# Gates applied ahead of the down product, expert rows added to x by accumulating DMAs, the sample tokens' out product in four column groups, and constant matmuls in the routing

## What is computed

```
pg = softmax(hf @ w_rg + b_rg); gi = argmax(pg); gp = pg[gi]
le_sel = (hf @ w_re + b_re).reshape(N, 4, 8)[gi]
top_p, top_i = top_k(softmax(le_sel), 2); top_p = top_p / sum(top_p)
gates = gp * one_hot(gi) * within(top_p, top_i)
a = einsum('nd,edf->nef', h, w_gate)
b = einsum('nd,edf->nef', h, w_up)
hid = silu(a) * b * gates[:, :, None]
moe = einsum('nef,efd->nd', hid, w_down)
y = rmsnorm(x + moe(rmsnorm(x, ln2_g)), lnf_g)
```

## Time and profile before

| | |
|---|---|
| median of 3 runs | 454.67 us (454.48 to 455.6) |
| profiled execution | 453.13 us |
| its span, first to last instruction | 451.2 us |
| mean granted TensorE clock | 0.929 |
| busy: PE, DVE, ACT, POOL | 378.4, 222.2, 151.7, 70.8 us |
| DMA | 109.14 MB, mean 242 GB/s |

### The profile page before, as it was taken

How to read it: one execution, slowest core, us unless ns; L and a number is a source line. 1 busy time by engine, 2 the same in 40 slices (tenths; PEclk the granted TensorE clock), 3 DMA queues, 4 the chain that set the end, 5 groups by cost and what they waited for, 6 DMA issues and landing times. The chain is left out here.

```text
span 451.2 us, 5978 instructions
## 1 busy us (share of the span) xinstructions
PE 378.4 (84%) x2256; PEld 193.8 (43%) x2256; DVE 222.2 (49%) x438; ACT 151.7 (34%) x322; POOL 70.8 (16%) x59
## 2 busy tenths in 40 slices
PE   1999996699799899999989999717999999999100
PEld 1554542244344334446544465515655555554000
DVE  2967356969765656347361234571122222222196
ACT  5823122034425436444441135502122222222042
POOL 0000303643350100000000000211233232221100
PEclk9999998889899999999999999956999999999655
DMA  8973321874900474910019996579999999995384
GB/s 292 361 210 98 138 93 52 269 267 140 368 27 0 134 249 143 295 69 2 1 49 397 410 410 271 202 276 388 358 395 410 412 410 409 408 403 229 129 332 170
DMA packets 42321, 109.14 MB, mean 242 GB/s; under 512 B 7864, under 2 KB 8632, under 8 KB 42288
## 3 DMA queue, kind: packets, MB, share of 16 engines
q1 hardware_dynamic: 36000, 94.78, 57.0%
q0 software_dynamic: 5856, 12.81, 7.7%
q10 hardware_dynamic: 432, 1.11, 0.7%
HBM read 100.00 MB, written 16.94 MB: 259 GB/s over the span
## 5 line engine op out<-in xcount | busy, mean ns | idle before, releaser
L1493 PE MATMUL bank<-weights_split,tokens_split 128*128 128x512 f16 (+1 forms) x744 | 175.1, 389 | 2.9 <-DVE x L1223 1.4
L1493 PEld LDWEIGHTS bank<-weights_split,tokens_split 128*128 128x128 f16 (+1 forms) x744 | 70.2, 98 | 94.7 <-issue 18.5
L620 POOL TENSOR_TENSOR big<-big,middle 128x1536 f32<-128x1536 f32 x8 | 28.2, 3531 | 100.4 <-DMA middle<-sample_q 50.9
L1764 PE MATMUL bank<-big,tokens_split 128*64 128x256 f32 x320 | 38.3, 394 | 1.6 <-ACT tokens_split L915 1.6
L1399 DVE TENSOR_TENSOR middle<-bank,middle 128x128 f32<-128x128 f32 x16 | 4.7, 293 | 58.5 <-ACT middle L920 58.5
L1764 PEld LDWEIGHTS bank<-big,tokens_split 128*64 128x64 f32 x320 | 23.6, 142 | 13.3 <-ACT tokens_split L915 2.1
L805 ACT ACTIVATE middle<-bank 128x128 f32<-128x128 f32 (+3 forms) x32 | 13.9, 434 | 38.2 <-PE bank L1541 37.9
L1468 PE MATMUL bank<-ident,big 128*128 128x128 f32 (+1 forms) x92 | 15.0, 299 | 13.8 <-DVE big L999 9.4
L989 DVE SCALAR_TENSOR_TENSOR weights_split<-middle,weights_split 128x1024 f16<-128x1024 f32 x16 | 19.0, 1220 | 13.1 <-ACT weights_split L720 13.1
L654 POOL DMA_INDIRECT tokens_split<-h_rows,middle x16 | 16.2, 1016 | 57.8 <-PE bank L1753 44.9
L636 POOL DMA_DIRECT2D h_rows<-middle x5 | 2.7, 537 | 135.8 <-ACT middle L886 135.8
(11 more groups left out here) (186 smaller groups left out, 506.9 us busy)
## 6 DMA issues: line engine op xcount, KB each, us to landing
big<-in_w_gate SPq DMA_DIRECT2D x10, 1024.0 KB
big<-in_w_up SPq DMA_DIRECT2D x10, 1024.0 KB
big<-in_w_down SPq DMA_DIRECT2D x10, 1024.0 KB
middle<-in_w_in SPq DMA_DIRECT2D x16, 512.0 KB, 6.0
big<-in_cache_win_k SPq DMA_DIRECT2D x24, 256.0 KB, 4.4
middle<-in_cache_win_v SPq DMA_DIRECT2D x24, 256.0 KB, 4.4
big<-in_w_out SPq DMA_DIRECT2D x8, 512.0 KB, 7.0
big<-expert_rows SPq DMA_DIRECT2D x8, 512.0 KB, 6.7
```

Source lines behind the costliest of these rows:

```text
L620: nc.gpsimd.tensor_tensor(prod[:, :, :], kring[:, b % 2], qb[:, b % 2, :].unsqueeze(1).to_broadcast([P, NPAT, W]), ALU.mult).then_inc(prod ...
L1493: ins = T.matmul(out, (hT if rows is None else rows)[:, high_low, k if rows is None else k - 4, tokens], wg[:, place, part, k, columns], s ...
L1764: ins = T.matmul((ptb, ovb)[b][e * CAP:(e + 1) * CAP, 0:2 * FE], xT[:, b, k, e * CAP:(e + 1) * CAP], places[slot][:, 0:2, e, k * FE:(k + 1 ...
```

## The change

- **Quarters.** The out product of the 8 sample tokens is split: four groups of two chunks each go to four groups of 32 columns of the array and so to four groups of PSUM partitions (`quarters_out`). ScalarE copies the bank to `partial`, and one float32 matmul with a constant `fold` adds the four (`quarters_sum`). The next tile's product stands between the two.
- **Constant matmuls.** `keep_on(36)`, `keep_on(20)` and `keep_on(20)` multiply constants into a PSUM bank that nothing reads, at three places of the routing.
- **Gates by slot.** The gates, split into two float16 parts, are brought from tokens to slots by ten more matmuls (`gate_sums`) and two VectorE steps (`slot_gates`), and `hidden` multiplies by them. `y2_dram` then holds rows with their gates.
- **Accumulating DMAs.** The ten row loads and `add_rows` go. POOL adds the rows of the first choice to `x_end` by one accumulating DMA for each tile, and, when it has landed, those of the second choice by another. ScalarE and VectorE wait for the second.

```diff
-                sp.dma_start(rows[0:n, t, k], y2_dram[at:at + n, :]).then_inc(rows_in[t], 16)
...
+            for t in LAST_ORDER:
+                pool.wait_ge(x_back[t], 16)
+                pool.dma_start(x_end[0:rows_of(t), t, :], dram_rows(y2_dram, t), accum_op=ALU.add).then_inc(first_added[t], 16)
+            for t in LAST_ORDER:
+                at = ROWS + t * P
+                pool.wait_ge(first_added[t], 16)
+                pool.dma_start(x_end[0:rows_of(t), t, :], y2_dram[at:at + rows_of(t), :],
+                               accum_op=ALU.add).then_inc(second_added[t], 16)
...
+            def copy_part(half):
+
+                n = UNIT[("part", half)]
+                act.wait_ge(acc_ready, n + 1)
+                nc.scalar.activation(partial, acc[n % 2][:, :], ACT.Copy).then_inc(free_a, 1)
...
-                act.wait_ge(mixed, i + 1)
+                act.wait_ge(second_added[t], 16)
...
+            step(V.tensor_scalar(gate_parts[:, 0, :], by_row, 16.0, None, ALU.mult))
+            step(V.scalar_tensor_tensor(out=gate_parts[:, 1, :], in0=by_row, scalar=16.0, in1=gate_parts[:, 0, :],
+                                        op0=ALU.mult, op1=ALU.subtract))
+            for v in range(2):
+                ins = V.tensor_tensor(gate_q[0][:, :, v, :], pair_hot, over_t(gate_parts[:, v, :], PAIRS), ALU.mult)
+            ins.then_inc(gates_split, 1)
             dve.wait_ge(cnt_ready, 1)
             step(V.tensor_reduce(r2[:, 0:1], acc[1][:, 256:256 + NE], AX, ALU.max))
             V.tensor_scalar(flag[:, :], r2[:, 0:1], float(CAP), None, ALU.is_gt).then_inc(flag_ready, 1)
...
+                dve.wait_ge(gates_summed, part + 1)
+                step(V.tensor_scalar(gate_of[:, a:b], tp[1][:, 0:m], 1.0 / 16.0, None, ALU.mult), chain)
+                step(V.scalar_tensor_tensor(out=gate_of[:, a:b], in0=tp[1][:, m:2 * m], scalar=1.0 / 16.0,
+                                            in1=gate_of[:, a:b], op0=ALU.mult, op1=ALU.add), chain)
...
-                V.tensor_tensor(hid[:, b], (ptb, ovb)[b][:, FE:2 * FE], sg[:, b], ALU.mult).then_inc(hid_done, 1)
+                V.scalar_tensor_tensor(out=hid[:, b], in0=(ptb, ovb)[b][:, FE:2 * FE], scalar=gate, in1=sg[:, b],
+                                       op0=ALU.mult, op1=ALU.mult).then_inc(hid_done, 1)
...
-            add_rows(LAST_ORDER[0])
-            for i in range(1, NT):
-                add_rows(LAST_ORDER[i])
-                final_norm(i - 1, LAST_ORDER[i - 1])
-            final_norm(NT - 1, LAST_ORDER[NT - 1])
+            for i, t in enumerate(LAST_ORDER):
+                final_norm(i, t)
...
+                for i, (high_low, part) in enumerate(((0, 0), (0, 1), (1, 0))):
+                    for j in range(2):
+                        for g in range(4):
+                            ins = T.matmul(acc[u % 2][32 * g:32 * g + NS, :], hT[:, high_low, 2 * g + j, SEQ:SEQ + NS],
+                                           wg[:, (5 + half) % 2, part, 2 * g + j, :],
+                                           start=i == 0 and j == 0, stop=i == 2 and j == 1)
...
+                T.matmul(acc[u % 2][0:NS, :], fold, partial, start=True, stop=True).then_inc(acc_ready, 1)
...
+            def keep_on(count):
+
+                for i in range(count):
+                    T.matmul(sbk[1][:, 0:2 * P], before_h, half_consts[:, :, :], start=True, stop=True)
+
+            pe.wait_ge(sq2, 2 * NT)
+            keep_on(36)
             pe.wait_ge(picks, 1)
```

More of the change, by code:

```diff
@@ L116, in constants @@
     c[r, C_BIND4 + r // 64 * 4 + r % 32 // HEADS] = 1
+    for b in range(NS):
+        c[b::32, C_FOLD + b] = 1
     return c
@@ L125 @@
 UNITS += [("u", NT - 1)]
-OUT_ORDER = [(t, h) for h in range(2) for t in TILES]
-UNITS += [("out", 2 * t + h) for t, h in OUT_ORDER]
+for _h in range(2):
+    UNITS += [("out", 2 * t + _h) for t in range(3)] + [("part", _h)]
+    UNITS += [("out", 2 * t + _h) for t in range(3, NT)]
 UNIT = {u: n for n, u in enumerate(UNITS)}
-BY_SCALAR = ("va", "v", "u")
+BY_SCALAR = ("va", "v", "u", "part")
 GROUP_AT = {"u": 0, "va": W, "q": 2 * W, "k": 3 * W, "v": 4 * W}
@@ L253, in build @@
         bindT = small[0:NS, o + HEADS + NS:o + HEADS + NS + NS * HEADS]
-        bind4 = small[:, C_BIND4 - C_M100:C_END - C_M100]
+        bind4 = small[:, C_BIND4 - C_M100:C_FOLD - C_M100]
+        fold = small[:, C_FOLD - C_M100:C_END - C_M100]
         qT = cut(big, 0, 4, SEQ)
@@ L391, in build @@
         zeroed = sem("zeroed")
+        gates_split, gates_summed, gate_copied = sem("gates_split"), sem("gates_summed"), sem("gate_copied")
+        second_added = [sem(f"second_added{t}") for t in range(NT)]
+        first_added = [sem(f"first_added{t}") for t in range(NT)]
         gu_in = [sem(f"gate_up_in{i}") for i in range(SLOTS)]
@@ L1663, in x_turns, with quarters_out, quarters_sum, project_out @@
                 turns(("h2", 2 * t + half), quarter(x[0:rows_of(t), t, :], half * 512))
-            def project_out(t, half, chunks=range(KD)):
+            def quarters_out(half):
+                u = UNIT[("part", half)]
+                free_wait(pe, u)
+                pe.wait_ge(w_split, PIECES * (6 + half))
+                wait_turned_out(pe, ("sgu", NT - 1))
+                pe.wait_ge(fin_copied, 1)
+                for i, (high_low, part) in enumerate(((0, 0), (0, 1), (1, 0))):
[4 more added lines that the diff above has]
+                                           start=i == 0 and j == 0, stop=i == 2 and j == 1)
+                ins.then_inc(acc_ready, 1)
+            def quarters_sum(half):
+                u = UNIT[("out", 2 * (NT - 1) + half)]
+                free_wait(pe, u)
+                left(pe, ("part", half))
+                T.matmul(acc[u % 2][0:NS, :], fold, partial, start=True, stop=True).then_inc(acc_ready, 1)
+            def project_out(t, half):
                 n = rows_of(t)
@@ L1688, in _ @@
             turns(("sgu", NT - 1), quarter(uu[0:NS, 4]))
-            for t in range(1, NT):
-                project_out(t, 0)
+            project_out(1, 0)
+            project_out(2, 0)
+            quarters_out(0)
+            project_out(3, 0)
+            quarters_sum(0)
             project_out(0, 1)
@@ L1705, in _ @@
             x_turns(2, 1)
-            project_out(NT - 1, 1, range(4))
+            quarters_sum(1)
             router(2, 0)
@@ L1746, in _, with gate_sums @@
             ins.then_inc(cnt_ready, 1)
+            keep_on(20)
+            def gate_sums(part, m):
+                pe.wait_ge(gates_split, part + 1)
+                for kt in range(2 * NT):
+                    n = rows_of(kt % NT)
+                    ins = T.matmul(tp[1][:, 0:2 * m], onehot_p[0:n, kt, :], gate_q[part][0:n, kt, :, :],
+                                   start=kt == 0, stop=kt == 2 * NT - 1)
+                ins.then_inc(gates_summed, 1)
+            gate_sums(0, PAIRS)
             def turn_x(n, b):
```

65 lines of the change are left out of this document (37 added, 28 removed).

## The result

The changed kernel takes 458.07 us (median of 6 runs, 456.92 to 458.83) against 455.26 us for the kernel before, measured beside it (6 runs, 454.48 to 456.22): a ratio of 1.0071, 95% interval 1.005 to 1.0092. It is **slower by 0.7%**; the forecast was 453.6 us, faster by 0.2%. The profiled execution took 456.92 us, with a span of 455.1 against 451.2 before.

A forecast was written before the change was run, and what follows sets the result against it. TensorE was taken as the bound ahead of a 26.4 us tail paced by VectorE. The front gains 5.3 us, the tail gives 4.2 back: span 450.1 against 451.2, 453.6 us from the median; range 443 to 464.

The forecast's parts named there:

- Quarters: 8-row out products ahead of routing: 2.2 us for 5.2 a half; last logits 3.4 us earlier, not 6.0.
- Constant matmuls: In the routing: the clock holds at full, so pair 1 comes a further 2.75 us earlier, together 6.2.
- Gates by slot: Behind the table: no cost in the pairs; 1.1 us of its steps stand ahead of the flag.
- Rival 3: In the routing: the clock falls all the same, some 5 us lost, 458; chance 0.07.
- The weight stream: Expert weight loads beside the pairs: they let pair 15 start 4.3 to 5.3 us earlier; 5.3 taken.
- the gap near 323 us: Stream gap where a down load waited for pair 0: closes, worth some 1.6 us.
- the slack: Between the last up weights' landing and TensorE's start on them: taken as 0 to 1 us.
- The tail's start and its stream: From last scatter landing at 419.5: 2.5 us to the first tile, then eight tiles in 20.0 us, to 442.0.
- c: Cost of one 512 KB accumulating tile in the tail: 2.5 us taken, between 1.25 and 5.0.
- The end: Last tile's square, root, reciprocal, product and store behind the last release: 6.15 us, as before.
- Rival 1: Tail: the second read is free, stream ends at 432.0, 443.6 us from the median; chance 0.18.
- Rival 2: Eight tiles after the last scatter: the accumulating stream becomes the bound, slower from c = 2.64; chance 0.20.

The follow-up runs named there:

- gates_and_tail: Kernel before with only the gates by slot and the accumulating DMAs, without quarters and constant matmuls: 460.77 us, ratio 1.0147.
- plain_rows: Changed kernel with its ten accumulating DMAs made plain copies on the same queue, leaving out those additions: 448.58 us, ratio 0.9884.
- some_accumulated: Changed kernel with row loads and VectorE additions back, 1 MB of pair 6's weights early, first choice of tiles 2 and 3 accumulated: 449.95 us, 0.9888.
- clock_kept: Changed kernel with row loads and VectorE additions back, 14 more constant matmuls before the last sample-row turns, 8 before the pairs: 451.78 us, 0.9937.

## Why the prediction was wrong

Forecast faster by 0.2%, measured slower by 0.7%. Its range (443 to 464 us) held the time. The span was to be 450.1 and is 455.1; the 5.0 us come from two terms.

*Quarters: right.* 1.47 us for the 24 matmuls (forecast 1.3) and 1.02 for the fold (0.9); VectorE went on at 282.42 (282.25), the logits ended at 287.46 (287.4). That the gain would be 3.4 and not 6.0, because the third row store is late next, was right (3.3).

*Constant matmuls: right in size at pair 1, by luck.* Pair 1 came 5.9 us earlier (forecast 6.2). But "I take it that the clock holds" is not so: it was at half from 285.3 to 288.7 and from 298.9 to 302.4. It happened to be back when pair 0 began; of the fourteen profiles with constant matmuls, pair 0's gate and up matmuls ran at full clock throughout in five. Rival 3 was there in part, at a small price.

*Gates by slot: no cost inside the pairs, as said.* The copy of pair 0 still waited 1.14 us for TensorE (4.78). Ahead of the flag they cost 0.9 us (1.1 taken), by gates_and_tail.

*The weight stream: the first step that failed.* I took -5.3 from bounds of 4.3 to 5.3, made of 2.65 us at the flag, 1.6 from the gap near 323 us and up to 1 of slack. The load behind the flag moved by 2.53 (300.94 against 303.47). But the gain tile, last of the stream, was issued 3.12 us earlier and landed after 17.9 us instead of 18.0: the whole stream moved by 3.2. So pair 15 moved by 3.1 and the last scatter by 3.2: **2.0 us** short.

Of these, 1.0 is the slack, which was nil. The prediction's own rows said so: 9 us ahead of the gain's landing at 420.8 is 411.8, which it read as "near 411", and TensorE began at 410.61. Another 0.9 is the gap, which moved the stream by 0.7 beyond the flag and not by 1.6. The gap itself did close, as the first window, of before, and the second, of the changed kernel, show:

```profile
324.00:328.00 4.00, 4.00 (x36) 2.51 (x34) 0.77 (x2) 0.76 (x2) 1.02 (x1) 1.00 0.99 330
...
324.00:328.00 4.00, 4.00 (x39) 2.68 (x36) 0.52 (x2) 0.52 (x3) 1.01 (x1) 1.00 1.03 413
```

The gathers and scatters of pairs that now run 5.9 us earlier pass through the same engines and may have taken the rest; no run here separates them from the weights. The sign to watch for was named (a wait of over 1 us ahead of pair 14 or 15); the size was not.

*The tail's start and its stream: the second.* c, the cost of one tile, was right at 2.5 us, and plain_rows shows that the accumulation makes it. Around it the sum was short by **3.0 us**, of which 1.9 lie ahead of the tiles. POOL saw the landing 4.8 us behind the issue (4.2 taken; over the profiles of these kernels it comes 2.9 to 5.0 us behind). It needed 1.8 us from there to its first issue (1.0 taken, as at the first gather; 0.7 of the excess is the flag's read), and each issue of a tile takes 0.85 to 0.9 (0.5 taken, from a row store). The other 1.0 lies in the stream: the engines moved only 111 GB/s from 426 to 428, and from 426, about where the tiles begin, to the last release are 23.0 us instead of 21.95. The end was right: 6.1 us from the last release (6.15). From the landing to the end the sum has 30.6 us (the prediction's list of signs says 30.5), and 33.0 were measured.

*The rivals.* Rival 1 (the second read is free, so that a tile costs what a plain one does) is excluded by 207 against 381 GB/s. Rival 2 had the right mechanism, a stream that bounds the tail, and the wrong condition: it was to decide from c = 2.64. That threshold leaned on the two other terms; with a front gain of 3.2 and 3.0 us more around the stream, the change loses at c = 2.5 already. With these, the break-even is 2.5 - 3.9 / 8, near 2.0 us a tile.

What stays open: which waiting makes the clock fall. Its falls move from one execution to the next: six executions of some_accumulated had spans from 445.0 to 449.7 us and mean clocks from 0.949 to 0.939, the longest at the lowest. That they go together is seen; that the clock causes all of it is not shown.

## What to carry to other kernels

An accumulating DMA moved about half of what a plain one did on the same queue (207 against 381 GB/s), and it lost as soon as its stream was what the end waited for. That it pays where the DMA engines idle beside a busy VectorE is only hinted at here, by some 0.8 us in one profile. A gain ahead of a stream of loads is worth what that stream itself moves up by: read it from the landing of its last load, not from the work that got faster. And before a gap in a DMA stream is filled, look whose short transfer passes through it.

## What was not expected

- With 3 MB of weights issued some 11 us ahead of it, a gather was waited for until 8.4 us after its issue; with 1 MB until 3.7 us after it, and without any until 3.3.
- The clock stood at half level in stretches that the constant matmuls kept busy: in the changed kernel TensorE was busy for 3.00 of 3.00 us from 299 to 302 at 0.50. What ran ahead of that stretch was sparse. Pair 15 of clock_kept, behind a wait of 1.97 us for weights, took 5.36 us instead of 3.67.
- POOL's addition held VectorE up for nearly its whole length: 2.35 us of work on POOL cost 2.2 us on VectorE. The two additions moved to POOL cost VectorE 4.3 us and saved it 2.5.
